# mLSTM mixer of a decoder trunk: the gates' maxima spread over the partitions by transfers through a DRAM buffer instead of TensorE products, the causal zeros set by GpSimd, scores and numerators one weight piece later

## The reference, cut to what matters

```python
qk = jax.nn.silu(causal_depthwise_conv(qk, conv_w))
log_i = (i_pre + b_igate);  log_f = jax.nn.log_sigmoid(f_pre + b_fgate)
b = jnp.cumsum(lf, axis=-1)
dmat = jnp.where(causal, b[..., :, None] - b[..., None, :] + li[..., None, :], -jnp.inf)
m_t = jnp.maximum(jnp.max(dmat, axis=-1), inter)
wt = jnp.exp(dmat - m_t[..., None])
s = jnp.einsum('bhtd,bhsd->bhts', qb, kb) * wt
num = jnp.einsum('bhts,bhsv->bhtv', s, vb) + ...
den = jnp.sum(s, axis=-1) + ...
h = num / jnp.maximum(jnp.abs(den), jnp.exp(-m_t))[..., None]
h = rmsnorm(h, head_gain)
return (jax.nn.sigmoid(o_pre) * h) @ w_out
```

## Time and profile before

| what | value |
|---|---|
| median of three runs | 1944.04 us |
| profiled execution | 1943.6 us |
| its span, first to last instruction | 1941.9 us |
| TensorE busy | 1922.5 us, 99% |
| VectorE, ScalarE, GpSimd busy | 1367.0, 1128.4, 64.3 us |
| mean granted TensorE clock | 0.998 |
| chain that ended last | 95% PE, 2% DVE, 1% ACT |

### The profile page before, as it was taken

One profiled execution on the slowest core, in us unless ns is written; L12 is line 12 of the kernel. 1 busy time (PEld: TensorE's weight loads), 2 busy tenths in 40 slices (PEclk: granted clock), 3 DMA queues, 4 the chain that ended last, 5 costly groups with the idle time before them and its releaser, 6 DMA issues.

```text
span 1941.9 us, 29533 instructions
## 1 busy us (share of the span) xinstructions
PE 1922.5 (99%) x10778; PEld 1657.6 (85%) x10778; DVE 1367.0 (70%) x1844; ACT 1128.4 (58%) x1678; POOL 64.3 (3%) x138
## 2 busy tenths in 40 slices
PE   8999999999999999999999999999999999999998
PEld 6888988888888888888888889888888888978887
DVE  6766776767776686676777776676677776767666
ACT  6555575555655566655565555765555556556553
POOL 2000000000100000000010001000000000000000
PEclk9999999999999999999999999999999999999999
DMA  6555534655555553455655554355556555535553
GB/s 219 194 194 196 174 131 137 210 194 193 165 192 190 170 195 130 154 194 194 208 175 192 186 172 124 130 174 194 194 173 204 186 185 178 172 125 166 192 194 119
DMA packets 244095, 343.35 MB, mean 177 GB/s; under 512 B 12077, under 2 KB 196026, under 8 KB 244026
## 3 DMA queue, kind: packets, MB, share of 16 engines
q1 hardware_dynamic: 242016, 340.29, 53.1%
q10 hardware_dynamic: 2010, 2.12, 0.5%
HBM read 340.27 MB, written 1.05 MB: 176 GB/s over the span
## 4 chain that ended last, share of the span: by engine, by line
PE 95%; DVE 2%; ACT 1%; DMA 0%; issue 0%; SPq 0%; ACTq 0%; POOL 0%; POOLq 0%; DVEq 0%
PE psum L532 33%; PE psum L695 33%; PE psum L703 17%; PE psum L990 5%; PE psum L563 1%; PE psum L1634 1%; DVE wlo L494 1%; PE psum L1032 1%; ACT whi L475 0%; PE psum L1691 0%; DVE mix L1181 0%; DMA raw<-in_ffn_wi 0%; PE psum L1043 0%; PE psum L1721 0%; PE psum L1668 0%
## 5 line engine op out<-in xcount | busy, mean ns | idle before, releaser
L475 ACT ACTIVATE whi<-raw,gains 128x512 fp32r<-128x512 f32 (+2 forms) x876 | 557.1, 709 | 266.5 <-PE psum L703 192.7
L695 PE MATMUL psum<-xT,whi 128*128 128x512 f32 x2816 | 678.6, 392 | 2.3 <-DVE wlo L515 1.9
L494 DVE SCALAR_TENSOR_TENSOR wlo<-raw,gains,whi 128x512 fp32r<-128x512 f32 (+2 forms) x876 | 596.8, 743 | 57.5 <-ACT whi L475 57.5
L695 PEld LDWEIGHTS psum<-xT,whi 128*128 128x128 f32 x2816 | 522.5, 188 | 111.2 <-issue 4.8
L703 PEld LDWEIGHTS psum<-xT,wlo 128*128 128x128 f32 x2816 | 344.3, 189 | 6.8
L703 PE MATMUL psum<-xT,wlo 128*128 128x256 f32 x2816 | 346.3, 281 | 0.0
L811 DVE TENSOR_TENSOR gate_in_T<-psum,low 128x512 f32<-128x512 f32 x88 | 60.9, 692 | 337.8 <-ACT low L758 337.4
L490 DVE TENSOR_TENSOR wlo<-raw,whi 128x2048 fp32r<-128x2048 f32 x100 | 228.5, 2285 | 43.7 <-ACT whi L471 43.7
L532 PE MATMUL psum<-wlo,hidT_hi 128*128 128x512 f32 x640 | 251.4, 393 | 0.0
L532 PE MATMUL psum<-whi,hidT_hi 128*128 128x512 f32 x640 | 249.0, 389 | 0.0
L532 PE MATMUL psum<-whi,hidT_lo 128*128 128x512 f32 x640 | 248.6, 388 | 0.0
(11 more groups left out here) (230 smaller groups left out, 1534.5 us busy)
## 6 DMA issues: line engine op xcount, KB each, us to landing
raw<-in_ffn_wi SPq DMA_DIRECT2D x350, 512.0 KB, 4.6
raw<-in_ffn_wo SPq DMA_DIRECT2D x176, 512.0 KB, 4.3
raw<-in_sb_w_in SPq DMA_DIRECT2D x48, 512.0 KB, 4.5
raw<-in_ml_w_in SPq DMA_DIRECT2D x24, 512.0 KB, 4.4
raw<-in_sb_w_out SPq DMA_DIRECT2D x16, 512.0 KB, 4.0
raw<-in_ml_w_out SPq DMA_DIRECT2D x8, 512.0 KB, 4.0
raw<-in_mla_w_out SPq DMA_DIRECT2D x8, 512.0 KB, 4.3
raw<-in_mla_w_in SPq DMA_DIRECT2D x4, 512.0 KB, 4.5
```

The lines of the kernel that those rows point to most:

```text
L475: last = act.activation(whi[:, slot, r], raw[:, slot, r], ACT.Copy, scale=gain_col(p.gain + k))
L494: last = dve.scalar_tensor_tensor(wlo[:, slot, p.at + r.start:p.at + r.stop], raw[:, slot, r], gain_col(p.gain + k), hi[:, r], op0=ALU.mul ...
L695: i = pe.matmul(psum[:, 4 + blk, :], whi[:, slot, k * 2 * FC + blk * P:k * 2 * FC + (blk + 1) * P], xT[:, 4 * part + k, :, :].rearrange("p ...
```

## The change

The row M goes another way: ACT stores the 8 rows of `g_M` in a DRAM tensor, waits for the store, and issues four transfers per group that each spread one row of 1 KB over 128 partitions, into `lw_rows` (in the place of `sel`). `exps(g)` reads these rows from SBUF with scale -1. The zeros above the diagonal are set afterwards by eight GpSimd selects per group. PE no longer has `log_weights`; `scores(0)`, `numerators(0)` and `scores(1)` stand one piece later, and the first two `y_fill` stand inside piece 12. `den`, `weigh`, `outputs` and all orders of DVE are as they were. In the set-up on GpSimd the fill of `g_M`, the fill of `sel` and its select are gone.

```diff
+        lw_dram = nc.dram_tensor("lw_dram", (ML_HEADS, SEQ), F32).ap()
-        sel, at = carve(at, ML_HEADS, P)
+        lw_rows, at = carve(at, GROUP, SEQ)
@@ ml_pe
-            def log_weights(g):
+            def scores(g):
+                pe.wait_ge(mqk_ready, 2)
                 if g:
                     pe.wait_ge(sw_done, g)
-                mask_pe(pe, 1, 0)
-                for hh in range(GROUP):
-                    pe.matmul(banks3(0)[:, KT0[hh]:KT0[hh] + SEQ], sel[:, GROUP * g + hh, :], g_M,
-                              start=False, stop=True, skip_group_check=True)
...
-            def scores(g):
-                pe.wait_ge(mqk_ready, 2)
-                pe.wait_ge(wt_done, g + 1)
                 scores_pe(pe, g, 0, mkT, mqT, True).then_inc(s_done, 1)
@@ order of ml_pe
             gates_back()
-            log_weights(0)
             piece(7)
             piece(8)
+            piece(9)
             scores(0)
-            piece(9)
+            piece(10)
             numerators(0)
-            log_weights(1)
-            piece(10)
             scores(1)
             piece(11)
             numerators(1)
-            y_fill(pe, s, 0, 0)
-            y_fill(pe, s, 1, 1, False)
-            piece(12)
+
+            def first_y():
+                y_fill(pe, s, 0, 0)
+                y_fill(pe, s, 1, 1, False)
+
+            piece(12, first_y)
@@ ml_act
             def exps(g):
-                act.wait_ge(lw_done, g + 1)
+                act.wait_ge(lw_spread[g], 16 * GROUP)
                 if g:
                     act.wait_ge(sw_done, g)
...
-                    act.activation(ml_wt[:, c:c + SEQ], banks3(0)[:, c:c + SEQ], ACT.Exp, bias=gate_T[:, 0, head:head + 1])
+                    act.activation(ml_wt[:, c:c + SEQ], lw_rows[:, hh, :], ACT.Exp, bias=gate_T[:, 0, head:head + 1],
+                                   scale=-1.0)
...
-                i.then_inc(wt_done, 1)
+                i.then_inc(wt_raw, 1)
+
+            def spread_rows(g):
+                if g:
+                    act.wait_ge(wt_raw, g)
+                for hh in range(GROUP):
+                    head = GROUP * g + hh
+                    act.dma_start(lw_rows[:, hh, :], lw_dram[head:head + 1, :].broadcast_to((P, SEQ))).then_inc(lw_spread[g], 16)
@@ order of ml_act
             act.wait_ge(gate_m, 1)
+            act.dma_start(lw_dram[:, :], g_M[0:ML_HEADS, :]).then_inc(lw_kept, 16)
             act.activation(g_em, g_t, ACT.Exp, scale=-1.0).then_inc(gate_em, 1)
             conv(8)
+            act.wait_ge(lw_kept, 16)
+            spread_rows(0)
             act.wait_ge(conv_done, 1)
             act.activation(mqT, q_out, ACT.Silu).then_inc(mqk_ready, 1)
             conv(9)
...
             exps(0)
             conv(10)
+            spread_rows(1)
@@ ml_set_up
-            pool.memset(g_M, 0.0)
-            link(pool.memset(sel, 0.0))
-            pool.affine_select(out=sel, in_=sel, compare_op=ALU.not_equal, fill=-1.0, base=0,
-                               pattern=[[-1, ML_HEADS], [0, P]], channel_multiplier=1).then_inc(pad_ready, 1)
@@ ml_pool
+            def causal(g):
+                pool.wait_ge(wt_raw, g + 1)
+                for c in (KT0[0], KT0[1], KT0[2], KT0[3], KT1[0], KT1[1], KT1[2], KT1[3]):
+                    i = pool.affine_select(out=ml_wt[:, c:c + P], in_=ml_wt[:, c:c + P], compare_op=ALU.is_gt, fill=0.0, base=1,
+                                           pattern=[[1, P]], channel_multiplier=-1)
+                i.then_inc(wt_done, 1)
+
+            causal(0)
+            causal(1)
```

More of the change, by code:

```diff
@@ L320, in trunk @@
         s_done = sem("s_done")
-        lw_done = sem("lw_done")
+        lw_spread = [sem(f"lw_spread{g}") for g in range(2)]
+        lw_kept = sem("lw_kept")
+        wt_raw = sem("wt_raw")
         wt_done = sem("wt_done")
@@ L1374, in exps @@
                     head, c = GROUP * g + hh, KT0[hh]
-                    act.activation(ml_wt[:, c:c + SEQ], banks3(0)[:, c:c + SEQ], ACT.Exp, bias=gate_T[:, 0, head:head + 1])
+                    act.activation(ml_wt[:, c:c + SEQ], lw_rows[:, hh, :], ACT.Exp, bias=gate_T[:, 0, head:head + 1],
+                                   scale=-1.0)
                 for hh in range(GROUP):
                     head, c = GROUP * g + hh, KT1[hh]
-                    i = act.activation(ml_wt[:, c:c + P], banks3(0)[:, c:c + P], ACT.Exp, bias=gate_T[:, 1, head:head + 1])
-                i.then_inc(wt_done, 1)
+                    i = act.activation(ml_wt[:, c:c + P], lw_rows[:, hh, P:SEQ], ACT.Exp, bias=gate_T[:, 1, head:head + 1],
+                                       scale=-1.0)
+                i.then_inc(wt_raw, 1)
[5 more added lines that the diff above has]
+                    act.dma_start(lw_rows[:, hh, :], lw_dram[head:head + 1, :].broadcast_to((P, SEQ))).then_inc(lw_spread[g], 16)
             def output_gate(half):
@@ L1562, in ml_set_up @@
             pool.memset(k_in[:, :, 0:3], 0.0)
-            pool.memset(g_M, 0.0)
             pool.memset(g_one, 1.0)
-            pool.memset(mv[:, :, :, P:P + 1], 1.0)
-            link(pool.memset(sel, 0.0))
-            pool.affine_select(out=sel, in_=sel, compare_op=ALU.not_equal, fill=-1.0, base=0,
-                               pattern=[[-1, ML_HEADS], [0, P]], channel_multiplier=1).then_inc(pad_ready, 1)
+            pool.memset(mv[:, :, :, P:P + 1], 1.0).then_inc(pad_ready, 1)
         def ml_pool(pool, link):
+            def causal(g):
[6 more added lines that the diff above has]
+            causal(1)
             for g in range(2):
```

## The result

| | before | after |
|---|---|---|
| median, us (11 runs each) | 1944.04 | 1949.72 |
| ratio after / before | | 1.0026 [1.0016, 1.0036] |
| profiled execution, us | 1943.6 | 1948.69 |
| its span, us | 1941.9 | 1947.0 |
| TensorE busy, us | 1922.5 | 1918.6 |

A forecast was written before the change was run, and what follows sets the result against it. TensorE was taken as the bound, busy 1922.5 of 1941.9 us. Profiled: 1943.6 - 6.4 removed + 9.5 gaps + 0.1 + 2.7 clock = 1949.5 us; plus 0.44 for the median, 1949.9; 8-in-10 range 1946.3 to 1952.8.

The forecast's parts named there:

- Credit: PE no longer runs log_weights(0) and log_weights(1), 3.2 us each: 6.4 us saved if nothing else moves.
- The 0.1 us for the split `y_fill`: y_fill inside piece 12 costs PE one more change between kinds of matmul: 0.1 us.
- First gap: Ahead of piece 7, which opens block 3, PE waits for DVE to read out tile 0 of block 2: 1.1 us.
- Second gap: Ahead of piece 9, which opens block 4, PE waits for DVE to read out tile 0 of block 3: 3.2 us.
- The term for GpSimd: Group 0's eight selects slow DVE's two-input work before it reads out block 3: 0.9 us, bounds 0 and 2.3.
- The sign that I had named: Single DVE instructions of the second convolution longer than 0.48 us beside the selects would show the forecast right.
- my upper bound: DVE's loss to group 0's selects if each whole 128x128 select stops it: 8 x 0.29 = 2.3 us.
- Third gap: Ahead of piece 11, which opens block 5, PE waits for ACT's sigmoid behind squares(0) to read out block 4: 5.2 us.
- Piece 11 later by 3.1: Piece 11, which started at 757.00 us before, starts 3.1 us later after the waits and the removed work.
- The clock: PE loses its clock once, in the wait ahead of piece 11: 2.7 us, bounds 0 and 5.4 for two falls.
- The issues on ACT: Store and four spreads cost ACT 0.68 to 0.73 us each, 2.8 us per group; conv(10) then ends just in time.
- The rival without a fall: PE waits at the three block changes but keeps its clock: 1947.2 us, chance 0.28.

The follow-up runs named there:

- the control: Kernel before, with the value blocks' first tiles read out ahead of the convolved piece and the output gate's sigmoid ahead of the squares: 1944.21 us, ratio 1.0001.
- late selects: Changed kernel, with GpSimd's selects of group 0 waiting until block 3 is read out: 1948.46 us in one profiled execution.
- early read-outs: Changed kernel, with DVE reading out tile 0 of blocks 2 and 3 ahead of conv(8) and conv(10): 1946.56 us, ratio 1.0012.
- the denser filler: Changed kernel, with 19 unread bf16 products of 512 columns between numerators(0) and scores(1) on PE: 1948.37 us, ratio 1.0019.

## Why the prediction was right

- **Credit, 6.4 us.** Right: the products are gone, and with every wait mended down to 1.7 us the kernel is 4.2 below before (the control excludes the repairs' own worth); some 0.5 us of the difference to 4.7 is the estimate given there. The 0.1 us for the split `y_fill` don't show: `numerators(1)` is 4.30 us later, the last `y_fill` 4.28.
- **First gap, 1.1:** 1.23, released by DVE's read-out as said.
- **Second gap, 3.2:** 2.27. The term for GpSimd in it, 0.9 us, was mis-sized: the shown cost on DVE is 0.14, and 0.16 by the late selects. In my one row of a meeting a DVE instruction was held by a single select of 1024 columns; here eight selects of 128 columns stood beside ten DVE instructions, and the selects waited. The sign that I had named, DVE instructions over 0.48 us, came only just: the six of the convolution have a mean of 0.498, in before 0.482. DVE went without idle time through the 3.88 us of the selects (2.06 alone) and lost 0.14, and all eight selects ran in them. So my upper bound, 2.3 us on DVE, was not one that this case came near.
- **Third gap, 5.2:** 5.26, by ACT's sigmoid, which follows `squares(0)` directly. Moving it took the gap away, and moving the scores and numerators took all but 1.60 of it.
- **Piece 11 later by 3.1:** 2.9, of which 0.3 comes from ahead of the mixer, so 2.6. The smaller second gap and these 0.3 us partly cancel.
- **The clock, 2.7:** one fall in the third gap, right in place; 1.4 us in the profile of after (6.97 against 5.57 for piece 11), 1.73 and 2.74 in two other profiles with the same wait. The price that I took from the start of the program was the upper end. (The windows of before show a granted clock of 1.00 over those 14 matmuls; it is the profiles of six other kernels here that show 0.50 from 14 to 16 us.) What decides it is how long PE runs at a granted clock of 0.50: about 3.0, 3.8 and 5.9 us in the three profiles, for 1.4, 1.7 and 2.7 us lost. Which wait is long enough for a fall was my estimate, and the runs show no one length: in before the windows have 1.00 up to 1936.5, 0.65 in the earlier trace rows and 0.50 from 1936.75 on, so it fell some 2.7 us after the last matmul had ended; in the waits of 5.3 us it fell 4.8, 2.2 and 4.3 us after PE stopped (after, late selects, early read-outs). That the second gap would keep its clock held for after, and failed in two of five profiles with a wait of 2.1 to 2.3 us.
- **The issues on ACT, 2.8 us per group, with "that cover is used up":** wrong in what they cost. They took 0.33 to 1.41 us each in the queue, but ran beside `conv(8)` and left ACT idle for 0.66 us, and ACT had the first part of its `conv(10)` done at 731.23, 2.4 us before DVE took it up, and not just in time. The spreads took 5.1 to 7.1 us to land, 5 were expected, and landed near 725.8, ahead of the 727 from which they would have been late.

The sum for the profiled execution was 1949.5, 0.8 above the 1948.69 measured: two terms too large (GpSimd by 0.8, the clock by 1.3), two left out (0.3 ahead of the mixer, 0.8 behind it, both within what single executions differ by), 0.2 of the gaps too small. The median stands 1.0 above the profiled execution and not 0.44, which is why it fits better than the terms do: that the forecast is 0.2 us from the median is luck. The other runs of after have a mean granted clock of 0.994 to 0.996, the profiled one 0.997, so more slow clock in them is likely, but no profile shows it. The rival without a fall, 1947.2, is excluded for the profiled run by its windows; as a median it is missed by 2.5 us. I had also overlooked that the kernel before has a stretch of low clock itself, at 1190 us. "No wait of PE in the middle of the trace is long enough to show a fall" looked only for waits: this fall came without one, while PE was shown busy, and it would have given a price for the middle of the trace.

## What to carry to other kernels

When work is taken from the bounding engine, look at what its old duration covered: here two read-outs on DVE and one on ACT were just in time, and 6.4 us of removed work came back as 8.8 us of waits. Work moved later on the bounding engine moves everything that hangs on it in the other engines' queues; a consumer queued behind such work (the sigmoid behind the squares) needs to be moved ahead of it; here that cost nothing in the wait of ACT that it filled, of which 1.99 us were left. A wait of 5.3 us lost the clock in all three profiles that have it, so it was worth its length plus 1.4 to 2.7 us. Waits of 1.8 to 2.3 us in the mixer did so in three of six, and those of 1.6 us and less in none. And compare two executions place by place before a group of runs is put down to one of them: the fall of the clock in the second gap, plain to see in the profile of the denser filler, was not what made that run slower.

## What the runs showed of the hardware that was not expected

- GpSimd beside two-input DVE work: eight 128x128 selects took 3.88 us instead of 2.06 to 2.18, while ten DVE instructions lost 0.14 us together. Single selects took 0.34 to 0.73 us there and 0.29 alone.
- The granted clock fell at PE waits of 5.25 us in every profile of such a wait (after, late selects, early read-outs), at 2.1 to 2.3 us in two of five, and at 1.81 in one. It also fell with PE shown busy, at about 1189.1 us in before, behind 20 products of one column. The same wait of 5.26 us cost 1.4 us in one execution and 2.74 in another. In the kernel with the late selects PE was already running again when it fell: it started at 735.76, the window from 735 to 736 has 1.00 and that from 736 to 738 has 0.60.
- Transfers issued on ACT behind a running instruction, 0.33 to 1.41 us each in its queue, let ACT's computing go on: four of them beside `conv(8)` left ACT idle for 0.66 us.
- Eight rows of 1 KB in two groups of four, each row spread over 128 partitions (128 KB), took 6.0 us to land in the median (5.1 to 7.1) beside the weights' stream, whose own pieces of 512 KB took 6.4 in that stretch.
